# Half blocks of the input projections between the attention groups of the second block

## The reference, cut to what matters

```python
    for l in range(DEPTH_2):
        u = rmsnorm(h, norm_mix[l])
        proj = u @ w_in[l]
        (qa, ka, va, qi, ki, wi, qb, kb, vb, qc, kc, vc, gc) = jnp.split(proj, split_pts, axis=-1)
        a_out = sparse_indexer_attention(...)     # 8 heads of 64, keys by the indexer's top 64
        b_heads = diff_attention(...)             # 4 heads, each p[:, 0] - lam * p[:, 1]
        b_out = (rmsnorm(b_heads, diff_norm[l]) * (1.0 - lambda_init)).reshape(bsz, t_len, B_W)
        ret = retention(qcr, kcr, ...)            # 4 heads, after rotary(qc), rotary(kc)
        c_out = jax.nn.silu(gc) * ret
        h = h + jnp.concatenate([a_out, b_out, c_out], axis=-1) @ w_out[l]
```

## Time and profile before

| | us |
|---|---|
| median of 3 runs (2875.14 to 2876.91) | 2876.8 |
| the profiled execution, its own time | 2878.41 |
| its span | 2876.6 |
| projections of the last four blocks, layer 0 and layer 1 | 51.7 and 51.7 |
| attention up to the first matmul of `po`, layer 0 and layer 1 | 121.3 and 107.2 |

### The profile page before, as it was taken

How to read it: one execution, slowest core, us unless ns; L and a number is a source line. 1 busy time by engine, 2 the same in 40 slices (tenths; PEclk the granted TensorE clock), 3 DMA queues, 4 the chain that set the end, 5 groups by cost and what they waited for, 6 DMA issues and landing times. The chain is left out here.

```text
span 2876.6 us, 43497 instructions
## 1 busy us (share of the span) xinstructions
PE 2601.1 (90%) x17640; PEld 1804.9 (63%) x17641; DVE 1256.7 (44%) x2888; ACT 861.8 (30%) x1829; POOL 158.1 (5%) x176
## 2 busy tenths in 40 slices
PE   7879999799989899989989989987878999978998
PEld 3767777476689543333333333337857999956998
DVE  3457776476646311111111111116745665654674
ACT  2335554122144111111111111114424355432453
POOL 0134433000000000000000000000000000000000
PEclk9799998898879899999999999998957999965999
DMA  6331110533046999999999999976402555410553
GB/s 199 57 72 40 51 39 2 164 117 117 15 136 197 374 409 409 409 409 409 409 409 409 409 409 409 409 291 201 129 1 70 165 174 164 135 50 26 173 183 117
DMA packets 257682, 601.82 MB, mean 209 GB/s; under 512 B 26082, under 2 KB 82633, under 8 KB 257481
## 3 DMA queue, kind: packets, MB, share of 16 engines
q1 hardware_dynamic: 256396, 598.56, 58.3%
q10 hardware_dynamic: 1085, 0.45, 0.1%
HBM read 594.56 MB, written 4.39 MB: 208 GB/s over the span
## 5 line engine op out<-in xcount | busy, mean ns | idle before, releaser
L2501 PE MATMUL banks<-moe_raw,moe_xs 128*64 128x512 f32 x2048 | 477.3, 605 | 31.8 <-DMA moe_raw<-in_w_gu 30.6
L2907 PE MATMUL banks<-xs_r,w_hi 128*128 128x272 f32 (+1 forms) x1632 | 474.5, 291 | 28.4 <-DVE w_raw_r L3329 19.8
L2911 PE MATMUL banks<-xs_r,w_raw_r 128*128 128x272 f32 (+1 forms) x1632 | 472.0, 289 | 0.0
L2908 PE MATMUL banks<-xs_r,w_hi 128*128 128x272 f32 (+1 forms) x1632 | 469.4, 288 | 0.0
L2907 PEld LDWEIGHTS banks<-xs_r,w_hi 128*128 128x128 f32 x1632 | 310.5, 190 | 33.6 <-issue 24.8
L3151 ACT ACTIVATE w_hi<-w_raw 128x512 fp32r<-128x512 f32 (+1 forms) x416 | 256.8, 619 | 244.4 <-PE banks L2911 200.0
L2501 PEld LDWEIGHTS banks<-moe_raw,moe_xs 128*64 128x64 f32 x2048 | 135.4, 137 | 304.2 <-issue 225.3
L2911 PEld LDWEIGHTS banks<-xs_r,w_raw_r 128*128 128x128 f32 x1632 | 310.5, 190 | 2.9
L2908 PEld LDWEIGHTS banks<-xs_r,w_hi 128*128 128x128 f32 x1632 | 311.0, 191 | 0.2
L2450 DVE TENSOR_TENSOR gu<-banks,vec 128x512 f32<-128x512 f32 x64 | 44.3, 692 | 604.8 <-PE banks L2531 604.7
L3329 DVE TENSOR_TENSOR w_raw_r<-w_raw,w_hi 128x512 fp32r<-128x512 f32 (+1 forms) x416 | 271.8, 677 | 55.1 <-ACT w_hi L3151 51.0
(11 more groups left out here) (489 smaller groups left out, 4008.3 us busy)
## 6 DMA issues: line engine op xcount, KB each, us to landing
moe_raw<-in_w_gu SPq DMA_DIRECT2D x256, 1024.0 KB, 18.5
moe_raw<-in_w_down SPq DMA_DIRECT2D x128, 1024.0 KB, 18.5
w_raw<-in_w_ff SPq DMA_DIRECT2D x256, 256.0 KB, 3.0
w_raw<-in_w_in SPq DMA_DIRECT2D x112, 256.0 KB, 2.7
gdn_w<-in_w_in SPq DMA_DIRECT2D x32, 512.0 KB, 4.1
mod_ring<-in_w_mod SPq DMA_DIRECT2D x16, 1024.0 KB, 5.2
ring_mod<-in_w_mod SPq DMA_DIRECT2D x4, 2048.0 KB, 20.0
wh<-in_w_in SPq DMA_DIRECT2D x8, 1024.0 KB, 9.5
```

The source lines that it names most:

```text
L2501: ins = pe.matmul(out if ph == "d" else out.rearrange("p (j x) -> p j x", x=P), x[:, 2 * q + k, :], w[:, c * 512:(c + 1) * 512] if ph == " ...
L2907: pe.matmul(bank, w_hi, x[:, 0, 0:n_cols], start=first, stop=False)
L2908: pe.matmul(bank, w_hi, x[:, 1, 0:n_cols], start=False, stop=False)
L2911: ins = pe.matmul(bank, w_lo, x[:, 0, 0:n_cols], start=False, stop=last)
```

## The change

Within each layer of the second block:

- The order of the blocks is QI, QB with KB, VB with QC, KC with VC, then QA, KA, VA, GC. The first four are projected whole, as before. The last four are cut in halves of two tiles each (seven halves, GC is one), in banks 0 and 1, and `HALVES` says in which turn of the attention's groups each half runs: three k steps, the second pass of scores, two k steps, the turn, three k steps, `weigh`.
- The rounding of these units (ACT), their low parts and the emptying of their banks (`half_out`, DVE) go into the turns too, and the rotary turn, most of the indexer's steps for tile 2 and the last 12 for tile 1 as well.
- The groups are ordered with branch B first. Scores have two banks (2 and 3) instead of four, in passes of two maps each (`passes`, `biased`).
- Branch A is divided by its sums before the transposes, by ACT (`normal`, one Copy with a scale per map), and its product has the values stationary: two heads in two column halves of the array, moving the 16 or 128 queries. The output comes out transposed, so branch A's half of `out_turn` and the copies L3288 go away; DVE copies bank 7 straight into `cat`. `x_first` of `po` waits for branch A only, and from k = 4 for the rest.
- Silu of the gate moves to the last turn but one.

```diff
-IN_BLOCKS = [(QI * P, 4, QI), (0, 4, QA), (4 * P, 4, KA), (8 * P, 4, VA), (COL2_B, 4, QB), (COL2_B + 4 * P, 4, VB),
-             (COL2_B + 8 * P, 4, KC), (COL2_B + 12 * P, 2, GC)]
-V_TILES = (VA, VA + 1, VA + 2, VA + 3, VB, VB + 1, VC, VC + 1)
+IN_BLOCKS = [(QI * P, 4, QI), (COL2_B, 4, QB), (COL2_B + 4 * P, 4, VB), (COL2_B + 8 * P, 4, KC),
+             (0, 4, QA), (4 * P, 4, KA), (8 * P, 4, VA), (COL2_B + 12 * P, 2, GC)]
+WHOLE = 4
+V_TILES = ((VB, 4), (VB + 1, 5), (VC, 6), (VC + 1, 7), (VA, 0), (VA + 1, 1), (VA + 2, 2), (VA + 3, 3))
+HALVES = ({-1: (4, 0), 0: (4, 1), 1: (5, 0), 3: (5, 1), 4: (6, 0), 5: (6, 1), 7: (7, 0)},
+          {-1: (4, 0), 0: (4, 1), 1: (5, 0), 2: (5, 1), 3: (6, 0), 4: (6, 1), 5: (7, 0)})
...
-    out = [(2, "B", 0, 4), (2, "B", 4, 4), (2, "A", 0, 4), (2, "A", 4, 4), (1, "B", 0, 4), (1, "B", 4, 4)]
-    if l < DEPTH2 - 1:
-        out += [(0, "B", 0, 8), (0, "A", 0, 8)]
+    first = l < DEPTH2 - 1
+    out = [(2, "B", 0, 4), (2, "B", 4, 4), (1, "B", 0, 4), (1, "B", 4, 4)] + ([(0, "B", 0, 8)] if first else [])
+    out += [(2, "A", 0, 4), (2, "A", 4, 4)] + ([(0, "A", 0, 8)] if first else [])
     return out + [(1, "A", 0, 4), (1, "A", 4, 4)]
+
+
+def passes(group):
+
+    t, br, _, ms = group
+    return [(0, 8)] if (t, br) == (0, "A") else [(j, 2) for j in range(0, ms, 2)]
+
+
+def index_steps(l):
+
+    rest = [(2, s) for s in range(8, IX_STEPS)]
+    later = [(1, s) for s in range(16, IX_STEPS)]
+    out = {("in", 3, k): [(1, s) for s in range(s0, s1)] for k, s0, s1 in
+           ((0, 0, 2), (1, 2, 4), (2, 4, 8), (4, 8, 10), (5, 10, 12), (6, 12, 14), (7, 14, 16))}
+    out.update({("in", 4, k): [(2, s), (2, s + 1)] for k, s in ((0, 0), (1, 2), (6, 4), (7, 6))})
+    n = 5 - l
+    each = len(rest) // n
+    for i in range(n):
+        out["slot", i - 1] = rest[i * each:(i + 1) * each]
+    for i in range(2):
+        out["slot", n - 1 + i] = later[i * 6:(i + 1) * 6]
+    return out
...
-                return ps.all[0:n, 0:4, 0:2 * w].rearrange("p b (s t) -> p s b t", s=2)
-            return ps.all[0:n, 0:4, 0:w]
+                return ps.all[0:n, 2:4, 0:4 * w].rearrange("p b (s t) -> p s b t", s=4)
+            return ps.all[0:n, 2:4, 0:w]
 
         def score_map(t, j):
-            return ps[j % 4][0:TT2[t][1], j // 4 * EXT[t]:(j // 4 + 1) * EXT[t]]
+            return ps[2 + j % 2][0:TT2[t][1], j // 2 * EXT[t]:(j // 2 + 1) * EXT[t]]
...
+                def half_step(l, b, h, k):
+                    n = at_u["in", l, b, k]
+                    w, last_half = IN_BLOCKS[b][1], 2 * h + 2 == IN_BLOCKS[b][1]
+                    pe.wait_ge(los, n + 1)
...
+                            before = ("in", l, b - 1, 2 * (b > WHOLE) + c) if h == 0 else ("in", l, b, c)
+                            pe.wait_ge(taken, done_t[before] + 1)
+                        w_hi, w_lo = hi[n % HI2][:, m * P:(m + 1) * P], rest[n % RING2][:, m * P:(m + 1) * P]
+                        bank = ps[c][:, 0:T2]
...
+                        if k == KT - 1:
+                            ins.then_inc(done, 1)
...
-                        m = m0 + j
+                    j0, nj = passes(GR[l][i])[h]
+                    if i or h:
+                        pe.wait_ge(ebias, part[l, i, h])
+                    for j in range(nj):
...
                     if br == "A":
-                        pe.wait_ge(exps, exp_n[l, i, ms - 1] + 1)
+                        pe.wait_ge(normed, grp_a[l, i] + 1)
                     else:
                         pe.wait_ge(combed, grp_b[l, i] + 1)
...
+                    if br == "A":
+                        for j in range(0, ms, 2):
+                            p = (m0 + j) // 2
+                            for st in range(t + 1):
+                                ns = TT2[st][1]
+                                for c in range(2):
+                                    ins = pe.matmul(ps[7][c * 64:(c + 1) * 64, p * P:p * P + n], vtok[0:ns, st, p * P + c * 64:p * P + (c + 1) * 64],
+                                                    PT[0:ns, i % 2, st, (j + c) * n:(j + c + 1) * n], start=(st == 0), stop=(st == t))
+                    else:
...
+                    later_scores(l, 0)
+                    pe.wait_ge(vt_a, 8 * l + 4)
+                    for i in range(4):
+                        ins = pe.matmul(ps[4 + i][:, 0:T2], con[:, K_ROT:K_ROT + P], pT[:, QC + i, :], start=True, stop=True)
+                        ins.then_inc(rot, 1)
+                    half_steps(l, -1, 5, KT)
                     for i in range(N):
+                        if i - 1 in turn_at[l]:
+                            pe.wait_ge(vt_a, 8 * l + turn_at[l][i - 1][1] + 1)
                         if i + 1 < N:
-                            scores(l, i + 1)
-                        if i < 4:
-                            if i == 0:
...
-                            retention(l, i)
-                            pe.wait_ge(at_v, 4 * l + i + 1)
-                        else:
+                            scores(l, i + 1, 0)
+                        if i:
                             pe.wait_ge(pt_v, grp[l, i - 1] + 1)
                             pe.wait_ge(pt_a, pt_a_at(l, i - 1))
+                        if 1 <= i <= 4:
+                            retention(l, i - 1)
+                        half_steps(l, i, 0, 3)
+                        if i + 1 < N:
+                            later_scores(l, i + 1)
+                        half_steps(l, i, 3, 5)
+                        if i == 0:
+                            pe.wait_ge(rot_v, 4 * l + 4)
+                        elif i <= 4:
+                            pe.wait_ge(at_v, 4 * l + i)
                         turn(l, i)
+                        if i in turn_at[l]:
+                            pe.wait_ge(ebias, part[l, i + 1, len(passes(GR[l][i + 1])) - 1] + 1)
+                            pe.wait_ge(taken, done_t["in", l, 6, 2 * (turn_at[l][i][0] > 4) + 1] + 1)
+                            for x in turn_at[l][i]:
+                                v_turn(l, x)
+                        half_steps(l, i, 5, KT)
                         if i:
                             weigh(l, i - 1)
                         if i in c_at[l]:
                             retention_out(l, c_at[l][i])
+                        if pend:
+                            finished(pend.pop())
                     pe.wait_ge(pt_v, grp[l, N - 1] + 1)
                     pe.wait_ge(pt_a, pt_a_at(l, N - 1))
-                    for j, (t, half) in enumerate(outs[l]):
-                        if (t, half) == (1, 0):
-                            weigh(l, N - 1)
...
+                def normal(l, i):
+                    t, br, m0, ms = GR[l][i]
+                    if br == "A":
+                        n, s = TT2[t][1], slot[t, br]
+                        e = e_of(i, t, ms)
+                        act.wait_ge(recs, grp_a[l, i] + 1)
+                        for j in range(ms):
+                            ins = act.activation(e[:, j, :], e[:, j, :], ACT.Copy, scale=rs[0:n, s, m0 + j:m0 + j + 1])
+                        ins.then_inc(normed, 1)
 
                 def turned_first(l, i):
...
+                def half_out(l, i):
+                    if i in HALVES[l]:
+                        b, h = HALVES[l][i]
+                        m0 = IN_BLOCKS[b][2]
+                        for m in (2 * h, 2 * h + 1):
+                            dve.wait_ge(done, done_t["in", l, b, m] + 1)
+                            dve.scalar_tensor_tensor(pT[:, m0 + m, :], ps[m % 2][:, 0:T2], A_SCALE if m0 == QA else 1.0, rinv[:, :],
+                                                     ALU.mult, ALU.mult).then_inc(taken, 1)
...
+                    else:
+                        x = rows[:, 8 + (m0 + j0) // 2:9 + (m0 + j0) // 2, :].broadcast_to([n, 2, EXT[t]])
+                    dve.tensor_tensor(by_bank(e, nj), src, by_bank(x, nj), ALU.add).then_inc(ebias, 1)
...
+                def inverses(l, i):
+                    t, br, m0, ms = GR[l][i]
+                    n, s = TT2[t][1], slot[t, br]
+                    dve.wait_ge(exps, exp_n[l, i, ms - 1] + 1)
+                    dve.reciprocal(rs[0:n, s, m0:m0 + ms], sm[0:n, s, m0:m0 + ms]).then_inc(recs, 1)
+
...
+                            inverses(l, i)
+                        if i + 1 < N:
+                            biased(l, i + 1, 0)
+                        if 1 <= i <= 4:
+                            decayed(l, i - 1)
+                        early(l, i, 4, 6)
                         if i + 1 < N:
                             front(l, i + 1)
-                        if i < 4:
-                            decayed(l, i)
-                        if GR[l][i][1] == "B":
-                            combine(l, i)
+                        else:
+                            head_sums(l)
+                        early(l, i, 6, KT)
+                        if i == 0:
+                            for x in range(4):
+                                rotary(l, x)
```

(46 more changed lines are left out.)

278 lines of the change are left out of this document (136 added, 142 removed).

## The result

| | before | changed |
|---|---|---|
| median, us | 2876.9 | 2838.9 (2834.6 to 2841.9) |
| ratio to before, 95% | | 0.9868 (0.9846 to 0.9891) |
| fifth block to `po`, both layers, us | 331.9 | 288.3 |

The account below looks back on a forecast made before the run. Attention was taken as a chain at half clock with no engine full. Filling its holes would cut the stretches from 173.0 and 158.9 us to 119 and 108, saving 105: 2772 us, range 2750 to 2822.

Parts of the forecast that it names:

- DVE becomes the fullest engine: In the stretches from fifth block to `po`, DVE busy 99.6 us in layer 0 and 92.1 in layer 1, PE 5 behind.
- No added wait there: Queues in the stretches: rounding of the next units waits only for slots that the half before frees; no added wait.
- Per turn one wait of about 1 us: In attention's turns, PE and DVE each stand for the other about 1 us: 10 us in layer 0, 8 in layer 1.
- about 2 us, inside that: Turn 0: PE waits about 2 us for four rotary turns, inside DVE's 4 to 5 us wait for the first exponentials.
- ACT's paragraph: ACT's work in layer 0: about 63 us, not the bound; `normal` puts 1.6 to 2.4 us in each A group's chain.
- The clock mostly full: Both stretches: TensorE's granted clock at the full level in most turns, near 0.9 or more; it carries half the saving.
- The product at 0: Branch A's product with values stationary: PE time changes by -9 to +18 us in layer 0, taken as 0.
- PE's sum: PE's work in the stretches at full clock: projections plus attention's matmuls, 95 us in layer 0 and 92 in layer 1.
- the factor of 0.55: Attention's own matmuls at full clock take 0.55 of their half-clock busy time: 88.0 us becomes 48 in layer 0.
- A turn of 11 us: An attention turn with a half block takes about 11 us (PE 10.7, DVE 10.0); one without takes 6 to 9.
- the first: Rival on the stretches: the clock falls in each turn and attention's matmuls stay at half; 2833 us, chance 0.13.
- the second rival: Rival on the turns: DVE's waits add up, 1.5 to 2 us more per turn over 18 turns; 2802 us, chance 0.17.

Follow-up runs that it names:

- e5: The changed kernel with three reorderings together: ACT's rounding earlier, retention outputs in banks 0 and 1, the head's order; 2790.3 us, ratio 0.9696 to the kernel before.
- e1: The changed kernel with ACT rounding the next four weight units and the output projection's first ahead of its copies of the transposes; 2809.4 us, ratio 0.9760.
- e2: The changed kernel with the retention's output matmuls written to bank 0 or 1 instead of bank 7; 2823.5 us, ratio 0.9817.
- e3: The changed kernel with scores 0's second pass ahead of three half-block steps and DVE's rotary turn ahead of group 1's front; 2829.6 us, ratio 0.9838.
- e4: The changed kernel without `normal`, so branch A's part of the result is not divided by its sums; 2831.8 us, ratio 0.9847.
- e8: e5 plus 46 unused float32 matmuls of 128x272 placed where PE waits; 2799.7 us, ratio 0.9730.
- e10: e5 plus DVE's late low parts ahead of its transpose copies, but each half block's products and low parts in one piece ahead; 2827.2 us, ratio 0.9836.
- e9: e5 plus DVE's late low parts ahead of its transpose copies and twenty unused matmuls where PE waits; 2789.8 us, ratio 0.9697.

## Why the prediction was wrong

- *The size of the miss*: the stretches are 61 us longer than summed (288.3 against 227). The three orders of e5 give back 39.3 of them, 29.7 of it idle time of PE and 9.6 busy time. In the other 22 PE is busy 33.6 us longer and idle 11.5 us less than summed.
- *Bound*: right that the attention was a chain at half clock with no engine full, and that the projections fill its holes. Wrong: **DVE becomes the fullest engine**. DVE was busy 94.3 and 87.3 us (99.6 and 92.1 forecast), ACT 58.2 (63); PE 120.6 and 109.5.
- *Rounding of the next units: "No added wait there"*: this is the step that failed most, and a wait put at nothing. I had looked at the slots and not at ACT's list, in which the late rounding stands behind `turned_first` and the exponentials. It cost 25 us in the stretches, 29.5 in the time (e1).
- *"Per turn one wait of about 1 us"*: I priced each turn as a sum of engines' work and did not ask of bank 7 who writes to it next. The wait of `retention_out`: 8 to 15 us (e2).
- *The head, "about 2 us, inside that"*: 5.3 us, since the rotary turn stood behind the second front on DVE, and the second pass of scores behind three k steps on PE (DVE waited 3.50 us for it); 7 to 9 us in both layers (e3).
- *`normal`*: named in ACT's paragraph as part of the chain, but with no term in the sum. 4 to 7 us, as a bound, since e4 removes its work too.
- *The clock mostly full*: 0.76 and 0.82 in the changed kernel, 0.79 and 0.88 without the three waits. Work at half pace is work lost: of e5's stretches (1 - 0.79) x 135.0 + (1 - 0.88) x 114.1 = 42 us, and with PE busy in 0.89 of them 37 of its busy time. That is an estimate, and it takes every matmul to last twice as long at the half level; with the 1.7 of the product's rows (5.00 against 2.95 us) it is 31. e8 shows 23 of it directly. The 33.6 us by which PE was busier than summed lie between the two.
- *The product at 0*: the near end of its bounds, -9, was the right one (-9.7 in layer 0, -10.8 in layer 1). It stood in PE's sum only, and I summed the stretches on DVE, so it explains nothing of the miss. But PE's sum at full clock comes out near all the same (220.6 less 31 to 37 is 184 to 190 us, against 187), so some 15 to 20 us of other matmuls were under-counted, in the factor of 0.55 or by being left out; which stays open.
- *A turn of 11 us*: in the reordered kernel e5 turns with a half take 11 to 15 us, from transposes to transposes (two of layer 1 11.3 and 11.5); in the changed kernel 11 to 23.
- *Rivals*: the time, 2839, is nearest to the first (2833), and not for its reason: PE was not at half pace throughout (120.6 us busy, not 145.5), and the three orders that cost 39 us of the stretches are of the second rival's kind, waits that add up. I had weighed the two as alternatives. They come together: in e10 waits and slower matmuls are added in about equal parts.

## What to carry to other kernels

Where work is threaded between the steps of a chain, write down for every engine what stands ahead of each instruction in its own list, also on the engine that seems to have time: here ACT, busy 58 of 153 us, cost more than the full ones, through a wait of DVE that PE's waits hardly show. Ask of each PSUM bank who writes to it next and how far down another engine's list its release stands. And don't price waits and the clock as rivals: where TensorE is the fullest engine, each microsecond of wait may cost about another in slower matmuls (18.7 and 16.9 us in e10).

## What the runs showed of the hardware

- Two heads in two column halves, with the values stationary and 128 queries moving: 24 records in 1.99 us at a granted clock of 0.98, 0.083 each, against 0.184 each for the old roles at 1.00. That is 2.2 times less. By the Trainium skill, "TensorEngine Tiling (Array Packing)", Theoretical Speedup, it is up to 2x; the drain at a change of tiling mode that its Key Properties name does not show as idle time ahead of the product (0.0 in its group above).
- The full level came back late: `po` in layer 0 began at half pace, and 4.7 us later its records were still 0.23 apart, where in the earlier trace rows they were at 0.29 each after 3.1 us.

```profile
2176.03 0.57 PE L2937 MATMUL banks<-xs_r,w_hi 128*128 128x272 f32 x1 [1.70 <-DVE xs_r L3436]
...
2180.47 0.43 PE L2938 MATMUL banks<-xs_r,w_hi 128*128 128x272 f32 x1
2180.70 0.42 PE L2941 MATMUL banks<-xs_r,w_raw_r 128*128 128x272 f32 x1
```

- Unused matmuls raised the granted clock from 0.79 and 0.88 to 0.91 and 0.94 (e8 against e5) and took 23 us off PE's own work, and yet didn't pay for themselves; twenty of them (e9) raised it in one layer and not in the other.
